# A hybrid decoder step on Trainium2: the sample tokens' own attention scores in seven pieces among the heads' softmax work on VectorE

## The reference, cut to what matters

```
s = einsum('nqhmd,nkhmd->nhmqk', q, k) * DK_B ** -0.5
p = softmax(where(mask, s, MASK_VALUE), axis=-1)
a = p[:, :, 0] - lam * p[:, :, 1]
o = einsum('nhqk,nkhv->nqhv', a, v)
```

## Time and profile before

| | us |
| --- | --- |
| median of 3 runs | 1011.26 |
| the runs | 1011.76, 1006.91, 1011.26 |
| the profiled execution | 1016.14 |
| its span in the trace | 1014.4 |
| TensorE busy | 914.7 (90%) |
| VectorE busy | 379.3 (37%) |
| ScalarE busy | 238.6 (24%) |
| GpSimd busy | 82.0 (8%) |
| mean granted clock of TensorE | 0.942 of full speed |
| mean share of the DMA engines, 700 to 850 us | 1.00 to 1.02 |

### The profile page before, as it was taken

How to read it: one execution, slowest core, us unless ns; L and a number is a source line. 1 busy time by engine, 2 the same in 40 slices (tenths; PEclk the granted TensorE clock), 3 DMA queues, 4 the chain that set the end, 5 groups by cost and what they waited for, 6 DMA issues and landing times.

```text
span 1014.4 us, 15620 instructions
## 1 busy us (share of the span) xinstructions
PE 914.7 (90%) x6377; PEld 483.5 (48%) x6377; DVE 379.3 (37%) x804; ACT 238.6 (24%) x600; POOL 82.0 (8%) x96
## 2 busy tenths in 40 slices
PE   6996999999999998978878994799999799798996
PEld 4453556655456875664345552344343234243442
DVE  5107545564226666254543225412111112111453
ACT  3116222220223322353212111100000000003344
POOL 1000000000014432000000000100000000002100
PEclk9998999999999999969778997799999899899999
DMA  6745233035347753065603705899999999995111
GB/s 218 301 156 169 40 145 146 1 145 181 145 128 240 238 181 99 4 230 153 204 0 120 291 23 226 309 375 366 402 396 383 390 406 401 401 344 176 44 41 45
DMA packets 71186, 209.55 MB, mean 207 GB/s; under 512 B 19113, under 2 KB 51332, under 8 KB 62540
## 3 DMA queue, kind: packets, MB, share of 16 engines
q1 hardware_dynamic: 56432, 185.53, 49.9%
q0 software_dynamic: 3936, 14.22, 4.3%
q10 hardware_dynamic: 10748, 8.80, 2.7%
HBM read 189.09 MB, written 38.26 MB: 224 GB/s over the span
## 4 chain that ended last, share of the span: by engine, by line
PE 76%; DMA 9%; DVE 7%; ACT 4%; issue 2%; SPq 1%; ACTq 0%; DVEq 0%; POOLq 0%
PE ps L2011 17%; PE ps L2423 10%; PE ps L2016 9%; PE ps L2316 6%; PE ps L2546 5%; PE ps L2460 5%; DMA EXPERT<-in_moe_w_up 4%; DMA aF<-in_moe_w_up 2%; PE ps L2048 2%; PE ps L2385 2%; PE ps L2419 2%; PE ps L2094 2%; PE ps L2175 1%; PE ps L2022 1%; PE ps L2121 1%
## 5 line engine op out<-in xcount | busy, mean ns | idle before, releaser
L2011 PE MATMUL ps<-xT,EXPERT 128*128 128x512 f32 x384 | 178.2, 609 | 0.5 <-DVE xT L1310 0.5
L2016 PE MATMUL ps<-EXPERT,xT 128*128 128x384 f32 (+1 forms) x384 | 120.7, 456 | 1.6 <-ACT EXPERT L974 1.6
L2011 PEld LDWEIGHTS ps<-xT,EXPERT 128*128 128x128 f32 x384 | 70.7, 193 | 76.3 <-issue 73.5
L2016 PEld LDWEIGHTS ps<-EXPERT,xT 128*128 128x128 f32 x384 | 78.2, 238 | 24.5 <-issue 3.5
L1913 DVE TENSOR_TENSOR dF<-dF,ps 64x512 f32<-64x512 f32 (+1 forms) x24 | 14.4, 601 | 163.1 <-ACT dF L1206 163.1
L2423 PE MATMUL ps<-EXPERT,wk 128*32 128x512 f32 x448 | 53.4, 621 | 7.8 <-DMA EXPERT<-in_moe_w_up 7.3
L2316 PE MATMUL ps<-EXPERT,xT 128*128 128x512 f32 x128 | 59.6, 618 | 0.8 <-ACT xT L1142 0.8
L2423 PE MATMUL ps<-EXPERT,samp 128*32 128x512 f32 x384 | 57.8, 594 | 0.0
L2546 PE MATMUL ps<-EXPERT 128*128 128x512 f32 x128 | 56.0, 594 | 1.3 <-DVE EXPERT L1966 1.3
L1210 ACT ACTIVATE dF<-ps 128x256 f32<-128x256 f32 (+1 forms) x24 | 8.4, 348 | 167.0 <-PE ps L2443 159.5
L1488 DVE TENSOR_REDUCE small<-ps 128x2 f32<-128x256 f32 (+3 forms) x24 | 19.8, 823 | 66.2 <-PE ps L2097 66.2
(11 more groups left out here) (472 smaller groups left out, 1301.9 us busy)
## 6 DMA issues: line engine op xcount, KB each, us to landing
EXPERT<-in_moe_w_gate SPq DMA_DIRECT2D x12, 2048.0 KB, 18.5
EXPERT<-in_moe_w_up SPq DMA_DIRECT2D x12, 2048.0 KB, 15.8
EXPERT<-in_moe_w_down SPq DMA_DIRECT2D x12, 2048.0 KB, 20.1
EXPERT<-in_w_in SPq DMA_DIRECT2D x13, 1536.0 KB, 6.7
out_win_sample<-in_cache_win SPq DMA_DIRECT2D x16, 1022.0 KB
aF<-in_cache_k_diff SPq DMA_DIRECT2D x32, 192.0 KB, 2.6
aF<-in_cache_v_diff SPq DMA_DIRECT2D x32, 192.0 KB, 2.5
Yd<-wk ACTq DMA_DIRECT2D x34, 128.0 KB
```

The source lines that it names most:

```text
L2011: last = t.matmul(ps[:, u % 2, :], W_[:, c, c0:c0 + w], xT[:, c, 0:SEQ], start=(c == 0), stop=(c == DC - 1))
L2016: last = t.matmul(ps[:, u % 2, 0:w], rows_, W_[:, c, c0:c0 + w], start=(c == 0), stop=(c == DC - 1))
```

## The change

`dec_new` takes a part number and is cut in seven (`NEW_PARTS = 4 + NG`, with `NG` = 3): part 0 the four tables, part 1 the scalars, part 2 the wait for the sample's unit and the 12 differential scores, parts 3 to 5 one dilated group each, part 6 the diagonal forms and the increment of `dec_row`. The arithmetic is the same, instruction for instruction. In the list, a part is put in behind every `d_t` from the same point on.

```diff
-    fresh = True
+    fresh = 0
...
-        if fresh and (not todo or todo[0][0] > summed[12]):
-            fresh = False
-            steps.append(("dec_new",))
+        if st[0] == "d_t" and fresh < NEW_PARTS and (not todo or todo[0][0] > summed[12]):
+            steps.append(("dec_new", fresh))
+            fresh += 1
...
-    if fresh:
-        steps.append(("dec_new",))
+    steps += [("dec_new", x) for x in range(fresh, NEW_PARTS)]
...
-            def dec_new():
-
-                dve.wait_ge(S_["unit_ok"], SUMU[12] + 1)
+            def dec_new(part):
+                if part == 0:
...
+                elif part == 1:
...
+                elif part == 2:
+                    dve.wait_ge(S_["unit_ok"], SUMU[12] + 1)
...
+                elif part < 3 + NG:
+                    g = part - 3
...
+                else:
...
+                    last.then_inc(S_["dec_row"], 1)
```

More of the change, by code:

```diff
@@ L75 @@
 NEW_FILL = 4
+NEW_PARTS = 4 + NG
 ORDER = (0, 1, 2, 4, 5, 6, 7, 9, 11, 8, 10, 12, 3)
@@ new lines, in dec_new @@
+            def dec_new(part):
+                if part == 0:
+                    seq(v.tensor_reduce(hms, ident[0:96, 0:96].rearrange("p (b r) -> p r b", b=NS), AX.X, ALU.add))
+                    seq(v.tensor_reduce(mB, ident[0:96, 0:96].rearrange("p (b r) -> p b r", b=NS), AX.X, ALU.add))
+                    seq(v.tensor_reduce(hsel, ident[0:32, 0:32].rearrange("p (b r) -> p r b", b=NS), AX.X, ALU.add))
+                    seq(v.tensor_reduce(mC, ident[0:32, 0:32].rearrange("p (b r) -> p b r", b=NS), AX.X, ALU.add))
+                elif part == 1:
+                    seq(v.tensor_reduce(st96[:, 3:4], hms.rearrange("p (h m) -> p m h", m=2)[:, 1:2, :], AX.X, ALU.add))
+                    seq(v.tensor_scalar(st96[:, 4:5], lam[0:96, :], 1.0, None, ALU.add))
+                    seq(v.tensor_tensor(st96[:, 3:4], st96[:, 3:4], st96[:, 4:5], ALU.mult))
+                    seq(v.tensor_scalar(st96[:, 3:4], st96[:, 3:4], -1.0, 1.0, ALU.mult, ALU.add))
+                elif part == 2:
+                    dve.wait_ge(S_["unit_ok"], SUMU[12] + 1)
+                    seq(v.tensor_tensor(dcst[:, 0:SLAB], samp[:, 4 * SLAB:5 * SLAB], samp[:, 5 * SLAB:6 * SLAB], ALU.mult))
+                    seq(v.tensor_reduce(snd, dcst[:, 0:SLAB].rearrange("p (r d) -> p r d", d=32), AX.X, ALU.add))
+                elif part < 3 + NG:
+                    g = part - 3
@@ L1561, in dec_new @@
                     seq(v.tensor_tensor(dcst[:, 0:256], samp3[:, g, 0], samp3[:, g, 1], ALU.mult))
                     seq(v.tensor_reduce(snc[:, g], dcst[:, 0:256].rearrange("p (r d) -> p r d", d=64), AX.X, ALU.add))
[L1563 to L1567, removed]
@@ L1568, in dec_new @@
-                last.then_inc(S_["dec_row"], 1)
+                else:
+                    seq(v.tensor_tensor(MD.rearrange("p (b r) -> p b r", b=NS), snd.unsqueeze(1).to_broadcast([NS, NS, 12]),
+                                        f2(ident[0:NS, 0:NS], 12), ALU.mult))
+                    for g in range(NG):
+                        last = v.tensor_tensor(MC[:, g], snc[:, g].unsqueeze(1).to_broadcast([NS, NS, HC]),
+                                               f2(ident[0:NS, 0:NS], HC), ALU.mult)
+                    last.then_inc(S_["dec_row"], 1)
```

## The result

The changed kernel took 1002.44 us (median of 13 runs, 996.68 to 1005.77), the kernel before 1011.26 (13 runs, 1006.91 to 1017.08). Ratio 0.9926, 95% interval 0.9898 to 0.9954: 7.5 us faster, between 4.7 and 10.3. The profiled execution took 1005.59 us, span 1003.8.

A forecast was written before the change was run, and what follows sets the result against it. The prediction took TensorE's stream as the bound. Stall 4.03, clock 1.7, slower transposes 0.1 and hidden pieces 0 made 5.8 us, taken from 1011.26: 1005.5 us, range 1001.5 to 1010.5.

The forecast's parts named there:

- The bound and the stall: TensorE idles 4.03 us before head 19's transposes: weigh(19) is held 7.6 us, less a margin of 3.6.
- 4.03 + 1.7 + 0.1 = 5.8 us: Gain at head 19: stall 4.03, slow clock behind it 1.7, slower first transposes 0.1 us.
- The pieces at nothing: The seven VectorE pieces of dec_new are hidden and cost 0; all seven exposed would cost 6.3 us.
- the gap of 1.51 us: VectorE's idle time before a later head's weigh, during ScalarE's exponentials; a piece of at most 1.15 us fits in.
- Head 19's margin: Without the hold, weigh(19) takes 1.70 us and ends at 387.0, 3.6 us before TensorE needs it.
- No later wait: Behind the stall TensorE does not wait anew; all behind 432 us slides with the stall.
- rival 3: A transfer after 432 us tied to an earlier time holds TensorE; 0 to 3.5 us remain; chance 0.12.
- rival 4: Clock falls more often in the dilated stage, 432 to 560 us, each 1.7 us; kernel slower; chance 0.05.
- rival 1: Stall only: in timed runs the clock seldom fell behind the stall; gain 4.1, time 1007.2 us; chance 0.16.
- rival 2: Slow stretch behind the stall twice as long in timed runs: gain 7.5, time 1003.8 us; chance 0.09.
- the clock's term: Matmuls right behind head 19's stall run partly at the lower clock level: 1.7 us, bounds 0 and 3.4.
- "Faster": Outcome that the whole kernel gains more than 0.5%, 5.06 us; given chance 0.56.

The follow-up runs named there:

- after: The changed kernel (seven pieces, wait moved to piece 2), main run against the kernel before: median 1002.44 us, ratio 0.9926.
- after_again: The changed kernel run once more, nothing altered: median 1002.9 us, ratio to the kernel before 0.994.
- filled: The kernel before with four unread 128x512 matmuls added ahead of TensorE's wait for head 19's weights: ratio to the kernel before 0.9985.
- block_at_20: The kernel before with all of dec_new, uncut and its wait ahead, moved two heads later behind d_t(20): median 1001.54 us, ratio 0.9934.
- split_only: The changed kernel with the wait for the sample's sums put back ahead of piece 0: median 1002.94 us, ratio to the kernel before 0.9954.
- split_memset_late: split_only with GpSimd's two zero fills made to wait for dec_row: ratio to the kernel before 0.9954.
- doubled: The changed kernel with every piece carried out twice, 6.3 us more VectorE work: ratio to the kernel before 0.9936.
- wait_only: The kernel before, block uncut at its old place, only its wait moved to just ahead of L1558: ratio to the kernel before 1.0007.
- block_at_22: The kernel before with all of dec_new in one piece four heads later, behind d_t(22): ratio to the kernel before 1.0005.
- block_at_22_again: block_at_22 run a second time, unaltered: ratio to the kernel before 1.0024.

## Why the prediction was right

- **The bound and the stall.** Right: the one idle time above 1 us in the differential stage went, and nothing took its place (`after`, `after_again`). That it was the hold on `weigh(19)` beyond TensorE's margin, neither the wait alone nor the block's length, is shown from three sides: the block with the wait moved stalls 2.93 us, the same block two heads later 0, four heads later 2.7.
- **4.03 + 1.7 + 0.1 = 5.8 us.** The stretch lost 5.94 in one pair of profiles and 5.96 in the other (49.13 - 43.17). The terms are shown one by one: `filled` takes the clock's part alone, 1.69; the remaining 4.25 are the idle time (4.03), the slower transposes (0.06) and an overlap that the sum left out (0.16: without a stall the transposes start at 387.17, and the matmuls ahead of them end at 385.14 + 2.19 = 387.33).
- **The pieces at nothing.** Right, with more room than I claimed: doubled they are free too. The argument from the gap of 1.51 us was sound but not needed; the margins alone carry an uncut block.
- **Head 19's margin.** The term that was off. I put `weigh(19)` at 1.70 us; beside GpSimd's products it took 384.74 - 382.07 = 2.67, and up to 3.25 in other profiles (`block_at_20`). It now ends 387.17 - 384.74 = 2.4 us ahead of the need, not 3.6; in `after_again` 2.1, in `block_at_20` 1.9. The forecast did not suffer, but in `split_only`, where the margin was thinner, the same effect left a stall.
- **No later wait.** No single run settles this, since each interval is nearly 3 us wide to either side. But the six sets of runs in which the stall is gone or under 0.4 us (`after`, `after_again`, `split_only`, `split_memset_late`, `block_at_20`, `doubled`) have ratios between 0.9926 and 0.9954, on average 0.9941: 6.0 us of 1009, for 5.4 to 5.9 in the stretch. (They share three sets of runs of the kernel before.) Rivals 3 and 4 found no support. For rival 3 the prediction named rows behind the stall; the DMA share in the stall itself, 390.6 to 394.6 us, was 0.00 as well.
- **Rivals 1 and 2, the size of the clock's term.** In two profiles of the kernel before the slow stretch was as forecast. Of the timed runs the profiles say nothing, and the 7.5 us of the main result is also rival 2's figure; its interval admits both. See what is open, below.
- **The time.** 1002.44 against 1005.5. The base of 1011.26 was the median of 3 runs and is also that of the 13 beside the changed kernel: the two medians of this result differ by 8.8 us, 3 more than forecast. The later sets of the kernel before (99 runs in all) have medians of 1008.5 to 1009.4, and 1009.0 - 5.8 = 1003.2, next to the 1002.44 and 1002.9 of the changed one. So the miss of 3 us is mostly a base that came out high; that 1002.44 is still inside the range, 0.9 us above its lower end, is owed to the allowance for scatter. "Faster" had 0.56 because the gain was 0.7 us over the line; both measured medians are over it, though the interval of each reaches below.

Open is the dilated stage. `wait_only` and `block_at_22` are 1.1 and 1.4 to 3.0 us better than before in the stretch and no better in time (1.0007, 1.0005, 1.0024). Take (1 - granted clock) x span as the time that a run loses to the lower clock, were TensorE always busy. Its mean over the runs is 59, 57 and 58 us in these three; the kernel before has 54, the changed one 51, `filled` 50. So the three lose more to the lower clock somewhere. Where and why, these runs don't show: only one execution of each is profiled, and that of `wait_only` (1005.25 us, 53 us lost) is not one that lost more. By the same means the change takes away 3 us and the filling 4, where the stretch shows 1.7; so part of the clock's gain may lie outside the stretch.

## What to carry to other kernels

Before cutting a block into pieces, work out for each place where it could stand when the next engine will want the result: one place with enough margin does as much as seven cuts, and a neighbouring place may bring the stall back. Count a stall of TensorE with the slow matmuls behind it, and read the gain first from the stretch that the change touches when whole runs scatter by more than the gain. Then check it against several sets of timed runs: here the gain in the stretch was found again in the times where the stall was gone, and was not where it was only shorter (`wait_only`, `block_at_22`).

## What the hardware showed that I had not expected

**VectorE and GpSimd hold each other up at SBUF.** Elementwise instructions of VectorE were stretched while GpSimd worked: L1503 0.75 to 1.64 us (`after`), L1502 0.49 to 1.96 (`split_only`), a product of 96x1 elements 0.16 to 1.16 (`wait_only`). GpSimd's timeline in the changed kernel shows the other side, L855 1.17 instead of 0.71 us:

```profile
382.74 1.45 POOL L854 TENSOR_TENSOR EXPERT<-EXPERT 128x512 f32<-128x512 f32 x1
384.15 1.17 POOL L855 TENSOR_TENSOR EXPERT<-EXPERT 32x256 f32<-32x256 f32 x1
```

L1503, begun at 383.10, ends at 384.74, which is 0.55 us after GpSimd's L854 (384.19), and 0.54 to 0.56 us after it in `after_again`, `block_at_20`, `block_at_22_again` and `doubled` too: it looks like waiting, then working, not like sharing. The reductions of part 0 beside GpSimd's L853 kept their lengths (the first 0.31 us, against 0.30 in `block_at_20`, where GpSimd was idle). And in the kernel before the product L1558 kept its 0.55 us beside GpSimd's first fill:

```profile
388.27 0.96 POOL L857 MEMSET EXPERT<- 128x1024 f32 x1
```

The Trainium skill (SBUF — State Buffer, Who interferes with whom) says that the two engines share a pair of ports which one instruction holds whole while the other blocks. It says that a VectorE instruction with two SBUF inputs contends with a GpSimd instruction that reads SBUF, not with one that only writes it; that `tensor_scalar` (L1502) can contend in its 2-port modes; and that reductions don't. These rows agree: L1503 and the products of `wait_only` were held up beside GpSimd's products, L1502 beside its fills, L1558 beside a fill was not, nor were the reductions. Which instruction was first can't be read here: in `split_only` L1502 starts 0.05 us ahead of the first fill and ends behind both. The prediction should have asked this of the weights' four instructions, since the change moved them 7.5 us earlier (2.8 instead of 10.3 us behind the start of their reduction), under GpSimd's last products.

**Stalls of 2.7 to 2.9 us let the clock fall too, but not each time.** After 2.93 us (`wait_only`) and 2.67 us (`block_at_22_again`) it fell at once, after 2.68 us (`block_at_22`) it did not; after 4.03 and 4.04 us (before) it did. The Trainium skill (TensorE: Matmul & The Clock Gate, Part 1) says that the window in which the chip judges activity is free-running and that the number of slow matmuls varies from run to run. For the shorter stall the two profiles of one kernel agree: the same four matmuls took 1.46 and 2.73 us.

**Most of the scatter between executions goes with the clock.** Over the 99 later executions of the kernel before, whose spans run from 1000 to 1021 us, the span and (1 - granted clock) x span have a correlation of 0.80. That is why a gain of 6 us is hard to see in a dozen runs.
